# One block for both attentions of layer 0, woven with linears, with a changed order of first tiles and modulation sums

## What is computed

```python
s_lat = where(valid, einsum('bkgqd,bksd->bkgqs', qb, kb) * scale, -inf)
s_ctx = einsum('bkgqd,bkcd->bkgqc', qb, k_ctx) * scale
p = softmax(concatenate([sink_col, s_lat, s_ctx], axis=-1), axis=-1)
o = einsum('...qs,...sd->...qd', p_lat, vb) + einsum('...qc,...cd->...qd', p_ctx, v_ctx)
```

## Time and profile before

| | |
|---|---|
| Three runs | 3328.7, 3337.9, 3337.1 us |
| Profiled execution: its own time | 3332.02 us |
| its span | 3330.2 us |
| mean granted TensorE clock | 0.938 of 2.4 GHz |
| busy | PE 89%, PEld 72%, DVE 38%, ACT 30%, POOL 30% |

### The profile page before, as it was taken

How to read it: one execution, slowest core, us unless ns; L and a number is a source line. 1 busy time by engine, 2 the same in 40 slices (tenths; PEclk the granted TensorE clock), 3 DMA queues, 4 the chain that set the end, 5 groups by cost and what they waited for, 6 DMA issues and landing times. The chain is left out here.

```text
span 3330.2 us, 38997 instructions
## 1 busy us (share of the span) xinstructions
PE 2964.7 (89%) x15588; PEld 2404.5 (72%) x15588; DVE 1252.2 (38%) x1869; ACT 1007.1 (30%) x1476; POOL 992.6 (30%) x482
## 2 busy tenths in 40 slices
PE   2789888578998999789998998999989999999998
PEld 1677787467887888668944776788758777887686
DVE  6456554563147116223013215611063554303523
ACT  2235544213311221331203223222243334324432
POOL 0130232112222222344301332444334433342343
PEclk7899999688999999889999998999999999999999
DMA  5200110231134116432210223432211110021121
GB/s 192 104 28 1 39 44 14 97 118 51 59 120 156 63 43 232 138 110 97 77 38 25 76 101 142 170 105 93 84 52 51 34 44 32 33 96 62 48 92 63
DMA packets 48957, 268.50 MB, mean 81 GB/s; under 512 B 5552, under 2 KB 6832, under 8 KB 28592
## 3 DMA queue, kind: packets, MB, share of 16 engines
q1 hardware_dynamic: 48816, 266.54, 22.9%
HBM read 264.42 MB, written 2.10 MB: 80 GB/s over the span
## 5 line engine op out<-in xcount | busy, mean ns | idle before, releaser
L413 POOL TENSOR_TENSOR shared_w_lo<-stage,shared_w_hi 128x2048 fp32r<-128x2048 f32 (+1 forms) x127 | 549.5, 4327 | 1392.0 <-ACT shared_w_hi L386 1392.0
L529 POOL TENSOR_TENSOR shared_w_lo<-stage,shared_w_hi 128x512 fp32r<-128x512 f32 (+2 forms) x233 | 301.2, 1323 | 516.1 <-ACT shared_w_hi L521 514.4
L386 ACT CAST shared_w_hi<-stage 128x2048 fp32r<-128x2048 f32 (+1 forms) x127 | 224.5, 1768 | 509.4 <-PEq L367 135.5
L453 PE MATMUL f0i_acc<-norm_b_hi,shared_w_hi 128*128 128x512 f32 x704 | 186.2, 346 | 26.1 <-DVE norm_b_lo L697 13.2
L453 PE MATMUL f0i_acc<-norm_b_lo,shared_w_hi 128*128 128x512 f32 x704 | 184.7, 344 | 0.0
L453 PE MATMUL f1i_acc<-norm_e_hi,shared_w_hi 128*128 128x512 f32 x352 | 140.1, 398 | 9.5 <-DVE norm_e_lo L697 8.0
L453 PEld LDWEIGHTS f0i_acc<-norm_b_hi,shared_w_hi 128*128 128x128 f32 x704 | 110.1, 193 | 45.1 <-issue 23.3
L596 PE MATMUL two_acc<-norm_f_hi,shared_w_hi 128*128 128x512 f32 (+1 forms) x312 | 131.7, 422 | 9.1 <-DVE norm_f_lo L697 9.1
L521 ACT CAST shared_w_hi<-stage 128x1024 fp32r<-128x1024 f32 (+2 forms) x117 | 114.6, 1023 | 82.6 <-PE last_acc L596 43.9
L453 PE MATMUL f1i_acc<-norm_e_lo,shared_w_hi 128*128 128x512 f32 x352 | 138.9, 394 | 0.0
L789 DVE TENSOR_TENSOR ffn_hidden<-f0i_acc,ffn_gate 128x512 f32<-128x512 f32 (+1 forms) x44 | 22.5, 552 | 307.4 <-PE f0i_acc L453 307.4
(11 more groups left out here) (544 smaller groups left out, 6983.0 us busy)
## 6 DMA issues: line engine op xcount, KB each, us to landing
stage<-in_w_f0i SPq DMA_DIRECT2D x22, 1024.0 KB, 4.9
stage<-in_w_f1i SPq DMA_DIRECT2D x22, 1024.0 KB, 4.8
mod_slots_d<-in_w_mod SPq DMA_DIRECT2D x32, 512.0 KB, 4.0
stage<-in_w_rv SPq DMA_DIRECT2D x16, 1024.0 KB, 4.9
mod_slots_a<-in_w_mod SPq DMA_DIRECT2D x24, 512.0 KB, 4.9
mod_slots_c<-in_w_mod SPq DMA_DIRECT2D x24, 512.0 KB, 3.5
stage<-in_w_rqk SPq DMA_DIRECT2D x12, 1024.0 KB, 4.9
mod_slots_e<-in_w_mod SPq DMA_DIRECT2D x24, 512.0 KB, 5.5
```

The costliest lines, as they stand in the source:

```text
L386: nc.scalar.copy(w_hi[:, slot, 0:size], stage[:, slot, 0:size]).then_inc(hi_ready, 1)
L413: nc.gpsimd.tensor_tensor(w_lo[:, slot, 0:size], stage[:, slot, 0:size], w_hi[:, slot, 0:size].bitcast(F32), ALU.subtract)\
L453: mm = nc.tensor.matmul(out[0:min(P, nt), b, 0:m], w[:, k, unit[1]:unit[1] + min(P, nt)], x[:, k, s:s + m], start=begin, stop=end)
L529: last = nc.gpsimd.tensor_tensor(w_lo[:, index % 2, part], stage[:, index % 2, part], w_hi[:, index % 2, part].bitcast(F32), ALU.subtract)
```

## The change

The stream order becomes bf0, bqg0, then bi0, bf1, bqg1, then bi1, bf2, bqg2, bf3, bqg3. The head norms are woven with bf0 and bqg0 alone (144 places), the attention with bi0, bf1 and bqg1 (216), the recurrence with bi1 and heads 2 and 3 (360), with other starts of its jobs.

**Attention.** Both attentions are one block of 24 pairs (6 query blocks, 4 pairs each; the pair's two heads use the two key heads). Queries and keys are read in place, without `q_zero` and without padding: each head uses its 64 rows. Blocks at the edge take two near blocks of keys, not three. The row is divided by its sum on VectorE ahead of the turn, and in the mixing the values are stationary (64 columns each, the two heads on different columns of the array), so that the result comes out turned and is copied straight to its place.

```diff
-            attend("win", LAT // P, [head_of(h, True) for h in range(8)], ...)
-            attend("ctxa", CTX // P, [head_of(h, False) for h in range(8)], ...)
+            line_w = chain([input_job(0)] + head_jobs(1), acc_w, ahead=True)
+            weights_of = [2 if m < 16 else 1 for m in range(PAIRS)] + [1, 1]
+            def pair_place(m):
+                return line_w["end"] * sum(weights_of[:m]) / sum(weights_of)
...
+                    def scores(m):
+                        i, c = divmod(m, 4)
+                        wait(pe, aw["scores_read"], 2 * m)
+                        def product(out, g, first, last):
+                            half = slice(64 * g, 64 * g + 64)
+                            return nc.tensor.matmul(out, qk[half, c, i * P:(i + 1) * P], k_rot[half, first:last],
+                                                    start=True, stop=True)
+                        if i < 4:
...
+                            for g in range(2):
+                                product(p_scores[g][:, 0:last - first], g, first, last)
+                            product(p_ctx[:, 0:CTX], 0, LAT, TOK).then_inc(aw["lat_scores"], 1)
+                            pe.wait_ge(aw["lat_scores"], m + 1)
+                            product(p_ctx[:, CTX:2 * CTX], 1, LAT, TOK).then_inc(aw["scores"], 2)
...
+                        for b, v in enumerate(blocks):
+                            for g in range(2):
+                                half = slice(64 * g, 64 * g + 64)
+                                mm = nc.tensor.matmul(p_mixed[half, 0:P], v_att[:, v, half],
+                                                      probs[:, (2 * m + g) % 4, b * P:(b + 1) * P], start=b == 0,
+                                                      stop=b == len(blocks) - 1, tile_position=(0, 64 * g))
...
+                    scores(0)
+                    for m in range(PAIRS + 2):
+                        more.upto(pair_place(m))
+                        if m + 1 < PAIRS:
+                            scores(m + 1)
+                        if 1 <= m <= PAIRS:
+                            turn(2 * m - 2)
+                            more.upto((pair_place(m) + pair_place(m + 1)) / 2)
+                            turn(2 * m - 1)
+                        if m >= 2:
+                            mix_values(m - 2)
```

```diff
-            begin_of = [60, 130, 200, start_of["bqg2"][0] + 54, start_of["bf3"][0] + 2, start_of["bqg3"][0] + 10] + [after] * 3
+            begin_of = [56, 100, 160, start_of["bqg2"][0] + 56, start_of["bf3"][0] + 24, start_of["bqg3"][0] + 22] + [after] * 3
```

**First tiles.** A linear with a chunked source and two units a tile (aq, eo, f0i0, ckv0, rqk, f1i0) takes its first tile chunk by chunk:

```diff
+                        def by_chunk(hi, lo, units):
+                            pe.wait_ge(hi_ready, ring.split + 1)
+                            for k in range(kc):
+                                pe.wait_ge(made["ready"], made["first"] + k + 1)
+                                for u, unit in enumerate(units):
...
+                                    for xi, x in enumerate((x_hi, x_lo)):
...
+                            pe.wait_ge(lo_ready, ring.tile + 1)
+                            for u, unit in enumerate(units):
+                                for k in range(kc):
...
+                                mm.then_inc(unit_done, 1)
```

```diff
-            return made["spread"](0, 16, 4, scale_ffn)
+            return made["beside"]([0] * 4, [6, 5, 5, 0], scale_ffn)
...
+            free = [2, 2, 2, 1, 1, 1, 1, 0]
...
+            return conds_c[0]["beside"]([1] * DC, free, conds_at="loaded")
+
+        def rest_of_next(scope):
...
+            return made["beside"]([0] * DC, [2] * 7 + [0], scale_mixer_1)
 
         def rest_of_layer_1(scope):
...
+            return made["beside"]([0] * 8, [4] * 6 + [0, 0], scale_ffn_1)
...
-        gate_linear("rg", n1_hi, n1_lo, qk_ret, ACT.Silu, ahead=True, source=ret_norm)
+        gate_linear("rg", n1_hi, n1_lo, qk_ret, ACT.Silu, ahead=True, source=ret_norm, side=rest_of_layer_1)
```

More of the change, by code:

```diff
@@ L377, in _ @@
                                 side["sp"](sp, t)
+                        if behind is not None:
+                            behind(sp)
                     @block.scalar
@@ new lines, in _, with exponent, copy_turned, copy_out @@
+                    more.rest()
+                @block.scalar
+                def _(act):
+                    more = Woven(line_w["act"](act))
+                    def exponent(n):
+                        act.wait_ge(aw["maximum"], n + 1)
+                        keys = row[:, n % 4, 0:keys_of(n // 8) + 1]
+                        nc.scalar.activation(keys, keys, ACT.Exp, bias=minus_max[:, n % 4:n % 4 + 1],
+                                             accum_out=total[:, n % 4:n % 4 + 1]).then_inc(aw["exp"], 1)
+                    def copy_turned(n):
+                        act.wait_ge(aw["turned"], n + 1)
+                        wait(act, aw["mixed"], 2 * (n // 2 - 1))
+                        nc.scalar.copy(probs[:, n % 4, 0:keys_of(n // 8)], p_turned[:, 0:keys_of(n // 8)])\
+                            .then_inc(aw["turned_read"], 1)
+                    def copy_out(m):
+                        i, c = divmod(m, 4)
+                        act.wait_ge(aw["mixed"], 2 * m + 2)
+                        nc.scalar.copy(mixed_0[:, c, i * P:(i + 1) * P], p_mixed[:, 0:P]).then_inc(aw["out_read"], 1)
+                    for m in range(PAIRS + 2):
+                        more.upto(pair_place(m))
+                        if 1 <= m <= PAIRS:
+                            copy_turned(2 * m - 2)
+                            copy_turned(2 * m - 1)
+                        if m < PAIRS:
+                            exponent(2 * m)
+                            exponent(2 * m + 1)
+                        if m >= 2:
+                            copy_out(m - 2)
+                    more.rest()
@@ L1521, in program, with _ @@
+                @block.gpsimd
+                def _(pool):
+                    Woven(line_w["pool"](pool)).rest()
         attn.close()
@@ L2132, in program, with gate_linear @@
         gates_done = [0]
-        def gate_linear(name, x_hi, x_lo, buf, func, other=None, ahead=False, source=None):
+        def gate_linear(name, x_hi, x_lo, buf, func, other=None, ahead=False, source=None, side=None):
             n = shapes[name][0]
```

392 lines of the change are left out of this document (170 added, 222 removed).

## The result

The changed kernel takes 3316.01 us (median of 7 runs, 3308.08 to 3322.39) against 3332.60 for the kernel before on the same chip (7 runs): ratio 0.9947, 95% interval 0.9930 to 0.9965. It is faster, by 17 us where I forecast 57 against the profiled execution. 3316 lies at the upper end of my range of 3240 to 3318, but less than a third of the forecast gain came. The profiled execution took 3322.39 us, 9.6 less than that of before.

A forecast was written before the change was run, and what follows sets the result against it. TensorE, busy 89% of the 3330.2 us span, was taken as the bound. Terms -17 + 20 - 28 - 16 - 9 - 8 - 2 + 3 = -57 from 3332.0 give 3275; forecast 3278 us, range 3240 to 3318.

The forecast's parts named there:

- Attention, +20: Attention block: 135 to 155 us, from 129 of pairs plus 26 of stalls, table loads, filling and ends; bounds 140 and 190.
- The mechanism of the halves: Attention: a pair's two heads on different rows or columns of the array overlap, so 20 mixing records take 1.4 us.
- rival B: Attention: halves don't overlap, mixing stays at 0.106 a record and scores at 1.13 a head; +19 us, 3294; chance 0.13.
- 7 of 14, 1.7 each, 12: Attention: 7 of 14 linear units end just before scores, so TensorE waits for copy and scores, 1.7 us each, 12.
- Rival C: Attention: GpSimd's 16 pieces hold VectorE's divisions in full through the shared port; +21 us, 3296; chance 0.09.
- Head norms, -17: Head norm block without bi0: ends at 222 against 239, 17 us less; bounds -10 and -22.
- Recurrence, -28: Recurrence: 192 matmuls leave (33 us of TensorE), but two of six intervals become too short; -28 us, bounds -33 and -12.
- Chunk order, -16: First tiles behind a norm: second unit's hi pass fills chunk waits in aq, f0i0, rqk, f1i0, ckv0; -16 us, bounds -8 and -20.
- Rival E: First tiles: chunk order does nothing, since tile 1's lo weights come late; 3291; chance 0.04.
- Modulation sums: Sums moved between stages: f0o0 -9, f0o1 -8, eo -2 (bounds -16, +5), rg +3 us (bounds 0, +12).
- four take 9.8, with 1.4 of gating 11.2: rg: four sums a tile with their DMA waits, plus gating, need 11.2 us of VectorE against TensorE's 11.1 a tile.
- Rival D: Modulation sums only move their cost: f0o0 -5, eo +5, rg +12; 3291; chance 0.08.

The follow-up runs named there:

- run 2: Changed kernel with useless transposes filling TensorE's waits in the attention block and the recurrence, waits kept: 3304.23 us, ratio 0.9892.
- run 1: Changed kernel with VectorE reading a pair's scores before it copies the linear's finished unit: 3287.23 us, ratio 0.9849, attention block 153.8 us.
- my fills: Useless transposes in TensorE's waits in the recurrence, on the changed kernel (3304.23 us, with attention fills too) and on it with three other edits (3276.42 us).
- run 8: Changed kernel with the first tile of every linear behind a norm in the earlier chunk order: 3330.25 us, ratio 1.0006.
- runs 3 and 4: Changed kernel with GpSimd's low parts in rg in four short instructions: ratio 0.9892; changed kernel with four column buffers in rg instead of two: ratio 0.9878.
- runs 6 to 8: Changed kernel with chunk order and sums both as before: ratio 0.9998; with only the sums as before: 0.9966; with only the chunk order as before: 1.0006.

## Why the prediction was right or wrong

**Attention, +20: wrong, 155 us forecast and 174.6 measured, 19.6 more.** The mechanism of the halves was right: 20 records of mixing take 1.24 from the first to the linear behind them, 0.062 each, where I had 1.4; rival B is refuted. The stalls were right, too: "7 of 14, 1.7 each, 12" against 8 and 13.3. What failed is that they were priced at their length alone. Some 8 us of the miss are the lower clock behind them (7 to 9 in run 2, 8.7 in run 1). The other 11 are left in run 1, whose 153.8 stand against 155 less the 12 of stalls. There, where nothing stalls, the eight pairs of three near blocks take 56.5 us from the first scores to the first of the next kind (241.53 to 298.01), 7.06 each where I had 6.75, and the four pairs of two near blocks behind them 6.4 to 7.0 where I had 6.1: 5 us together. The other 6 lie at the ends: the first four pairs, the context pairs and what follows them take 70 where my parts came to 64 (in all three profiles the clock is low for 10 us at the block's start, and I had nothing for that). One pair of three near blocks in run 1, its scores and first transposes:

```profile
276.50 0.92 PE L1398 MATMUL attend_scores<-k_rot,qk 64*128 64x384 f32 x4
...
278.59 0.77 PE L1418 MATMUL attend_turned<-ident,attend_row 128*128 128x128 f32 x5
```

From scores to transposes 2.09 us pass where I had 1.9. The transposes take 1.16 (1.1), the mixing 1.24 (1.4), the two pieces of linear 2.75 (2.35), 7.23 in all: what was short is the linear's piece above all, with the step from one kind of work to the next in it.

Rival C had GpSimd hold the divisions in 16 pieces (they are 12); the block's first two do take 0.81 and 1.32 instead of 0.49, but GpSimd is busy 15.3 us in the whole block, and run 1 reached 153.8 with it in place: not the cause.

**Head norms, -17: right.** 61.3 us from the first linear to the first scores, 80.2 before; the forecast had 59.

**Recurrence, -28: the mechanism right, the size wrong.** -16.9 in the profile, -20 by the mean of ten. "318 places in place of 458" holds, and with the two split intervals at their fast values (28.4, 28.1) the changed kernel's 248.1 would be 237.9, my 237; no profile has both (the lowest is 241.6). The step that failed is that the shorter recurrence would keep the clock of the longer. My sum had no term for it. Its clock is 0.78 to 0.83 in ten profiles where it was 0.87 in one. That less linear work under the same waits is the reason is argued, not shown. Why a given run keeps the clock in one interval and loses it in the next stays open, too; my fills did not settle it.

**Chunk order, -16: right in sign and place, low in size.** 20 by run 8 (20.7 by its stages), at the end of the bounds I gave: aq gave 6.3 and not 4.2, rqk 4.3 and not 3, ckv 2.7 and not 1.6, f1 4.2 and not 3, f0 3.2 and not 4.4. Rival E is refuted.

**Modulation sums.** f0o0 and f0o1: -17 forecast, -17.3 measured; of the holes of 13 and 12 us, 2 and 4 are left. eo: -2 forecast, -3.5 measured. rg: +3 with bounds 0 and +12, measured +22.7, beyond the bound. The step that failed is in the working itself: "four take 9.8, with 1.4 of gating 11.2", against 11.1 of TensorE, which left nothing to spare, and then "I take nothing" for GpSimd's hold, a sentence written for the attention block and not worked out for rg, although had the 5.46 and the Trainium skill's rule stood beside them. One hold of 4 a tile in six tiles is 24 us, on a tile with no room left; runs 3 and 4 show that without the holds, or without the waits for loads, the tile fits. Rival D, which had sums only move, was right in mechanism for rg and had 12 where it is 23. (Its own parts add to +20, 3295, not to the 3291 that it gives; the range holds either.)

**The sum.** -57 forecast. At the level of runs the change is -17 to -18, and runs 6 to 8 split it: the block 0 (good to 6), the chunk order -20, the sums -6 (each good to 8), so that they need not add exactly. The range held, by its end; my forecast's chance of 0.44 stood on a sum in which every stage kept the high clock.

## What to carry to other kernels

Price a short wait of TensorE by what follows it as well: here eight waits of 1.7 us on the average cost about 1.1 more each in the matmuls behind them, all of it behind half of them. Where a change takes work from a stretch and leaves its waits, look at that stretch's granted clock afterwards: the recurrence had 0.79 where it had been 0.87. In a woven block, let the engine first do what TensorE waits for next and only then copy what is merely finished; moving that one line took 20.8 us off its block, more than the whole change gave (17). Before work is put beside a linear, add up the receiving engine's tile: the sums, their loads and the holds by GpSimd in series, against what TensorE takes for a tile, and look for a stage where nobody waits for that engine.

## What was not expected of the hardware

- The clock falls behind waits as short as 1.75 us and stays low for 3.4 to 6.9 us of nearly full work (five transposes 1.33, then 0.71). The length of the wait alone does not decide it: ahead of one group of transposes TensorE waits 2.4 us in the changed kernel and 2.6 in runs 1 and 2, and the clock falls behind it in the first two, not in run 2. Behind the wait of 2.1 us ahead of a head's outputs in the recurrence it stays at 0.50 from 499 to 513 with TensorE busy throughout, as here:

```profile
505.00:510.00 5.00, 5.00 (x26) 5.00 (x25) 0.00 (x0) 0.00 (x0) 0.00 (x0) 0.50 0.00 0
```

- Work without use made a block faster: 84 transposes, 174.6 to 165.0 us.
- The same recurrence takes 241.6 to 250.3 us in ten profiles, and where two of its intervals differ most, the difference lies in how long TensorE's records are.
- When GpSimd's one long instruction is cut in four, the sums wait less and GpSimd more: 1.70 us in the median for an instruction of 512 columns in rg, against 1.28 in the attention block of the changed kernel.
